# Sampled keys of a paged latent attention: turned by VectorE in 32x32 blocks and scored by 32x32 tiles of TensorE, with work moved between ScalarE, VectorE and GpSimd

## The chip, the core and the metric

The kernel runs on one core of a Trainium2 chip. The metric is the device time of one execution in microseconds (us). A core has TensorE (PE, matmuls and its weight loads, PEld), VectorE (DVE), ScalarE (ACT), GpSimd (POOL) and SyncE (SP), each with its own queue of instructions; they wait for one another through semaphores. PSUM has 8 banks of 512 fp32 values in each of 128 partitions; the kernel calls them K[0] to K[3] and Q[0] to Q[3].

## What is computed

Two layers of a decoder step on 1024 prompt tokens and 8 sequences of 4 sampled tokens. Each layer has latent attention (MLA, 8 heads), an RWKV-7 recurrence (4 heads of 64), a short convolution, an output projection and a mixture of 32 experts. Everything is fp32. The sampled tokens of sequence b attend to 8192 past keys, held in pages of 128 keys with a latent of 128 numbers and a rotary part of 32. Cut to what this change touches:

```python
# sampled attention: ql (8 x 4 x 8 x 128) and qr (.. x 32) against the paged cache
ckv_past = ckv_pages[page_table].reshape(bd, -1, MLA_KV_RANK)   # 8 x 8192 x 128
kr_past = kr_pages[page_table].reshape(bd, -1, MLA_ROPE_DIM)    # 8 x 8192 x 32
s_past = (einsum('bqhc,bkc->bhqk', q_lat, ckv_past)
          + einsum('bqhr,bkr->bhqk', q_rope, kr_past)) * ATTN_SCALE
pr = softmax(concatenate([s_past, s_new], -1), -1)
out = einsum('bhqk,bkc->bqhc', pr[..., :n_past], ckv_past) + ...
# short convolution of the prompt, per channel, width 3
padded = concatenate([buf0, gate_c * u], 1)
y = gate_b * sum(conv_w[j] * padded[:, j:j + t_] for j in range(3))
# recurrence, output side: per-head norm of y, times gain, plus the bonus
bonus = sum(r * k * r_k, -1) * v
out = (yn * lnx_g + lnx_b + bonus) * g
```

## The kernel before

A layer has a projection, a first slot for the sampled rows' recurrence, then eight slots, then the output projection, routing and experts. Slot b does three things at once: the rest of prompt tile b's recurrence, the sampled attention of sequence b, and, from the seam on, prompt tile b+1's preparation together with prompt tile b's causal attention. Its **end** (`end_of_slot`) runs first: TensorE interleaves the last parts of the recurrence (off1, off2, mv, off3, wt, u, st) with the sampled attention. Then comes the **seam** (lora, mlaT, gate and so on of the next tile), then the **body** (`slot`): eight heads of the prompt's scores s0 to s7, with their exponentials, transposes and products, between the steps of the next recurrence. The causal attention grows with the tile, so slot 0 takes about 60 us and slot 6 about 82 us. "Slot 3" below means the stretch from the first sampled key turned for b=3 to the first for b=4. The order on each engine is written out by hand.

The sampled attention of one b is four groups g of 2048 keys, gathered by GpSimd into `ckvr[g]` (128 rows of 16 keys each). In each group:

- TensorE transposes 16 blocks of 128x128 (`keys`, "k0" to "k15" over the four groups), ScalarE copies the results out of Q[1] and Q[2] to kT, 512 columns at a time (`keys` on ScalarE).
- TensorE multiplies the rotary keys (krT, turned by VectorE in 32x32 blocks from krr, step r) by a block diagonal query (qrbd) into Q[0], and adds eight products of the latent query (qcurs, 128x32) with 256 keys each, in four column tiles of 32 (`scores`, step s).
- VectorE adds the window, takes the row maximum (step s), joins it with the earlier maximum across the four column tiles (m), ScalarE takes the exponential (e), VectorE turns the result in 32x32 blocks (T), TensorE multiplies by the values (v), and VectorE accumulates (o).

On VectorE the same stretch holds, of the next tile, kk (the key scaled and squared), of this tile z (two operations that make the bonus and the norm's bias, L2470), u0, u1 and y (copies out of PSUM, L2862 and L2920), off1 (two copies, L2804 and L2805), off3, rows, st, and the prompt tile's convolution (`conv_first`, `conv_rest`: seven operations on 128x256 values). In the body it holds for each head the scores' maximum and a small second instruction, negm (L2974), which multiplies it by minus the scale for ScalarE's exponential; and the grams, masked two heads at a time in 128x128 operations. GpSimd holds roots (rstd and the like), and the gathers of pages and rotary keys: `later_pages` brings the fourth page group and, once VectorE has turned the first two groups' rotary keys, the last two's.

## Time and profile before

| what | us |
| --- | --- |
| runs (three) | 2938.42, 2931.49, 2927.01 |
| median of the runs | 2931.49 |
| span of the profiled execution | 2909.1 |
| TensorE busy | 2670.6 (92%) |
| VectorE busy | 1358.0 (47%) |
| ScalarE busy | 799.2 (27%) |
| GpSimd busy | 648.3 (22%) |

The profiled execution is known by its span only, from its first to its last instruction; the median of the runs is 22.4 us above that. A busy share is a mean over stages: TensorE's 92% says that it is the engine to look at first, not that it sets the time everywhere. The recorded line of a matmul is that of a helper (L964, transposes L961), and that of most two-operand operations of VectorE is L2470, so the names of the operands tell which step is meant. An fp32 matmul leaves two records, a transpose one. "128*32" is the tile of TensorE in rows and columns, "128x256" the moving operand.

### The profile page before, as it was taken

To read this page: it belongs to the slowest core of one execution; us is meant where nothing else is said; L and a number is where in the kernel's file an instruction comes from. 1 tells how busy PE (TensorE), PEld (TensorE's weight loads), DVE (VectorE), ACT (ScalarE), POOL (GpSimd) and SP (SyncE) were. 2 spreads that over 40 slices of the span, in tenths; PEclk is the share of its full clock that TensorE was granted. 3 is DMA by queue.
4 is the path that set the end of the run, shared out by engine and by line. 5 is a ranking of instruction groups with operands and counts; after the bars stand their busy time and mean duration, and the time that the engine had idled before them with its cause. 6 is when DMAs were issued, how large, how long until landed. Compare 5 with 4: busy or idle time off the path is not lost.

```text
span 2909.1 us, 56004 instructions
## 1 busy us (share of the span) xinstructions
PE 2670.6 (92%) x22234; PEld 1459.2 (50%) x22234; DVE 1358.0 (47%) x3828; ACT 799.2 (27%) x1905; POOL 648.3 (22%) x664
## 2 busy tenths in 40 slices
PE   7999899999999959999599998999999997799996
PEld 4445666666655523333244456666666554233332
DVE  4313777666643552222451247677665536322224
ACT  0111455555532101111111014555555210011113
POOL 1000211111100045555320001111111000555543
PEclk9999999999999969999799998999999998899998
DMA  7112433332242549999661133334322326599985
GB/s 299 74 37 53 163 101 109 115 99 83 83 152 81 216 156 360 365 360 329 231 231 58 35 106 116 124 98 121 98 94 80 144 75 265 196 364 357 363 307 209
DMA packets 171814, 502.23 MB, mean 173 GB/s; under 512 B 48388, under 2 KB 89608, under 8 KB 146344
## 3 DMA queue, kind: packets, MB, share of 16 engines
q1 hardware_dynamic: 105624, 321.28, 32.1%
q0 software_dynamic: 50240, 120.23, 12.1%
q10 hardware_dynamic: 15696, 57.15, 4.9%
q8 instruction: 181, 2.97, 0.4%
q14 instruction: 73, 0.60, 0.1%
HBM read 629.15 MB, written 86.89 MB: 246 GB/s over the span
## 4 chain that ended last, share of the span: by engine, by line
PE 78%; DVE 10%; DMA 3%; ACT 3%; DVEq 2%; issue 2%; POOL 0%; POOLq 0%; SPq 0%; ACTq 0%
PE ps L964 70%; PE ps L961 8%; ACT PT L1924 1%; DVE S_all L2972 1%; DVE grams L2470 1%; DMA xd<-o_x 1%; DMA c_x<-xd 1%; ACT S_all L2206 1%; DVEq L2973 1%; DMA l_b<-ybd,dga 1%; DVE negm L2974 0%; DVE uu L2470 0%; DVE krT L2995 0%; DVE r_e L2470 0%; DVE t L2470 0%
## 5 line engine op out<-in xcount | busy, mean ns | idle before, releaser
L964 PE MATMUL ps<-w_slots,xbT 128*64 128x512 f32 (+1 forms) x2048 | 457.4, 599 | 19.0 <-DVE xbT L3429 19.0
L964 PE MATMUL ps<-hT,w_in 128*128 128x512 f32 x896 | 392.0, 595 | 1.2 <-ACT hT L1924 1.2
L867 POOL DMA_INDIRECT xb<-xd,idall x256 | 256.1, 1000 | 144.7 <-issue 80.4
L964 PEld LDWEIGHTS ps<-w_slots,xbT 128*64 128x64 f32 x2048 | 144.0, 138 | 286.7 <-issue 267.4
L964 PEld LDWEIGHTS ps<-hT,w_in 128*128 128x128 f32 x896 | 167.9, 190 | 203.3 <-issue 199.9
L3429 DVE STREAM_TRANSPOSE xbT<-xb 128x1024 f32<-128x1024 f32 x64 | 79.7, 1245 | 357.2 <-DMA xb<-xd,idall 355.0
L964 PE MATMUL ps<-w_out,o_mixT 128*128 128x512 f32 (+1 forms) x640 | 240.0, 555 | 1.4 <-DVE o_h L3235 1.3
L964 PE MATMUL ps<-w_slots,hidT 128*64 128x512 f32 (+1 forms) x1024 | 231.8, 593 | 4.7 <-ACT hidT L1924 2.6
L1924 ACT ACTIVATE kT<-ps 128x512 f32<-128x512 f32 x256 | 138.5, 593 | 128.0 <-PE ps L961 128.0
L964 PE MATMUL ps<-grams 64*64 64x64 f32 (+1 forms) x3536 | 143.1, 228 | 21.9 <-DVE grams L2470 20.0
L964 PE MATMUL ps<-kcat,qcat 96*128 96x512 f32 (+3 forms) x384 | 154.4, 511 | 8.4 <-DVE negm L2974 8.4
L961 PE MATMUL ps<-cst,S_all 128*128 128x128 f32 x832 | 137.7, 285 | 19.8 <-ACT PT L1924 15.7
L964 PEld LDWEIGHTS ps<-w_slots,hidT 128*64 128x64 f32 x1024 | 80.0, 137 | 145.6 <-issue 136.9
L799 POOL TENSOR_TENSOR lnt<-lnt,cst 128x1 f32<-128x1 f32 x36 | 37.3, 1036 | 517.3 <-DVE lnt L2479 517.3
L964 PEld LDWEIGHTS ps<-w_out,o_mixT 128*128 128x128 f32 (+1 forms) x640 | 97.9, 175 | 106.6 <-issue 101.4
L2530 DVE TENSOR_SCALAR stage<-ps,omu 128x512 f32<-128x512 f32 x32 | 24.0, 749 | 270.8 <-PE ps L964 270.8
L1924 ACT ACTIVATE PT<-ps 128x512 f32<-128x512 f32 (+3 forms) x208 | 102.2, 491 | 170.7 <-PE ps L961 132.4
L964 PEld LDWEIGHTS ps<-grams 64*64 64x64 f32 (+1 forms) x3536 | 123.3, 140 | 50.3 <-issue 37.8
L2972 DVE CUSTOM_DVE_ANT_0 S_all<-ps,window 128x256 f32<-128x256 f32 (+7 forms) x128 | 96.5, 754 | 104.9 <-PE ps L964 104.8
L2206 ACT ACTIVATE S_all<-S_all,negm 128x256 f32<-128x256 f32 (+7 forms) x128 | 98.9, 773 | 153.2 <-DVE negm L2974 153.0
L1924 ACT ACTIVATE yb<-ps 128x512 f32<-128x512 f32 x64 | 38.2, 597 | 367.7 <-DMA ybd<-yb 319.6
L961 PEld LDWEIGHTS ps<-cst,S_all 128*128 128x128 f32 x832 | 91.8, 141 | 72.7 <-ACT PT L1924 33.7
(439 smaller groups left out, 4088.4 us busy)
## 6 DMA issues: line engine op xcount, KB each, us to landing
w_slots<-in_w_gu SPq DMA_DIRECT2D x64, 2048.0 KB, 12.6
w_slots<-in_w_dn SPq DMA_DIRECT2D x64, 1024.0 KB, 6.8
ybd<-yb ACTq DMA_DIRECT2D x64, 512.0 KB, 8.3
pd<-stage SPq DMA_DIRECT2D x56, 256.0 KB, 2.5
w_in<-in_w_in SPq DMA_DIRECT2D x6, 2048.0 KB, 24.4
out_y<-c_h ACTq DMA_DIRECT2D x18, 512.0 KB, 2.8
o_mixT<-mixd SPq DMA_DIRECT2D x18, 512.0 KB, 3.7
xd<-o_x ACTq DMA_DIRECT2D x18, 512.0 KB, 2.8
```

The costliest lines, as they stand in the source:

```text
L799: return pool.tensor_tensor(x, x, mh.to_broadcast(shape), ALU.pow)
L867: pool.indirect_dma_start(xb[p % 2][:, 256 * q:256 * q + 256], None, x_quarters, bass.IndirectOffsetOnAxis(ap=idall[:, NE * q + p:NE * q + ...
L961: return pe.transpose(out, in_, ident[s, s])
L964: return pe.matmul(out, lhsT, rhs, start=start, stop=stop, skip_group_check=True)
L1924: return act.activation(out, in_, ACT.Copy)
L2206: self.done(act.activation(S_sb[h % 2][:, :keys], S_sb[h % 2][:, :keys], ACT.Exp, bias=negm[:, h:h + 1], scale=SCALE, accum_out=den[:, h:h ...
L2470: return dve.tensor_tensor(out, x, y, op)
L2530: dve.tensor_scalar(dst[:], src, omu[:, f:f + 1], None, ALU.mult)
L2972: dve.tensor_tensor_reduce(S_sb[h % 2][:, :keys], src, window[:, SEQ - keys:], 1.0, LOW, ALU.add, ALU.max, m8[:, h:h + 1])
L2973: dve.drain()
L3429: dve.transpose(xbT[p % 2][:].rearrange("p (c i t) -> p i c t", c=8, i=4), xb[p % 2][:].rearrange("p (i c t) -> p i c t", c=8, i=4)).then_ ...
```

## The change

The sampled keys are no longer transposed by TensorE. VectorE turns each group's 128x2048 values in 32x32 blocks, in two instructions of 128x1024 (`keys`, steps K0 to K3), into one of two buffers: `kTb0`, or the upper half of `grams`, which the recurrence's matrices leave free because they are laid out anew at 256 columns each. A block turned this way has its 32 latent numbers in one of four row groups of TensorE, so the latent query is held in four shifted copies (`qblk`, made once per layer by sixteen small matmuls and two ScalarE copies, step rep), and a group's scores are 40 matmuls of 32x32 tiles with 256 moving columns: five per output tile (four latent blocks c and the rotary part), over four row tiles j and two halves a. The half a goes to bank Q[a] and to column tile (j + 2a) mod 4. ScalarE's sixteen copies per b are gone. Since the keys' order in half 1 is shifted by two column tiles, VectorE turns the exponentials in three instructions instead of one.

The maxima become minima of the scores times minus the scale, so that negm and its scaling are gone; the masked grams are taken four heads at a time. The prompt tiles' convolution and bonus go to GpSimd (`conv`, `bonus`), kk, u0, u1, y and one copy of off1 to ScalarE. The buffers that the convolution and the grams used change, and with them what SyncE waits for before it loads conv inputs and `w_out` in the last slot (`OUT_GROUPS`). The sampled rows' own convolution stays on VectorE.

The diff, cut:

```diff
-DVE_SATT = "r0 r1 s0 m0 T0 r2 s1 m1 r3 o0 T1 s2 m2 o1 T2 s3 m3 o2 T3 o3".split()
...
+DVE_SATT = "s0 m0 T0 s1 K2 m1 r2 o0 T1 s2 m2 K3 r3 o1 T2 s3 m3 o2 T3 o3".split()
+DVE_ATT = "1s0 1s1 1s2 2K0 1s3 1s4 1s5 1s6 2K1 1s7 1rden 1a 2r0 2r1".split()
+DVE_SATT0 = "r0 K0 r1 K1".split()
...
+        gD, gDT, gN, gM, gX, gXT, gR, gRT, gB, gK = X
+        qrep = grams[:, 4608:4864].rearrange("p (b q) -> p b q", b=NB)
+        kTb = [kTb0[:], grams[:, 2048:4096]]
         wukT = grams[0:64, 0:8 * KR]
...
+            def conv(l, i):
...
+                pool.tensor_tensor(cvp, cvp, cvx[:, 2:4], ALU.mult)
+                pool.drain()
+                pool.tensor_tensor(cvy, cvp[:, :, 0:P], pf(V_CW), ALU.mult)
+                for j in (1, 2):
+                    pool.tensor_tensor(cvt, cvp[:, :, j:j + P], pf(V_CW + 2 * j), ALU.mult)
+                    pool.drain()
+                    pool.tensor_tensor(cvy, cvy, cvt, ALU.add)
+                    pool.drain()
+                pool.wait_ge(mixC_out, 16 * n)
+                pool.tensor_tensor(mixC[:, 2:4], cvy, cvx[:, 0:2, LEAD:], ALU.mult).then_inc(pool_a.sem, pool_a.mark(k, "conv"))
...
+            def bonus(l, i):
...
+                pool.wait_ge(act_a.sem, act_a.at(k, "mv"))
+                pool.tensor_tensor(mix[:].rearrange("p (h v) -> p h v", h=RH), tokm[:, 0:2, :].rearrange("p f (a v) -> p (f a) v", a=2), bc(bon[:], [P, RH, 64]), ALU.mult)
+                pool.drain()
+                pool.tensor_tensor(mix[:], mix[:], rows[:, R_LXB:R_LXB + 256], ALU.add).then_inc(pool_a.sem, pool_a.mark(k, "z"))
...
+                conv(l, b)
                 pool.wait_ge(dve_b.sem, dve_b.at(k, "r0"))
                 ropes(l, b, 2)
                 pool.wait_ge(dve_b.sem, dve_b.at(k, "r1"))
...
+                        pe.wait_ge(dve_b.sem, dve_b.at(("satt", self.l, self.i - 1), "s3"))
                     decay, iclr = (Q[1], Q[2]) if self.seam else (K[1], K[3])
...
+                def scores(self, g, part):
...
+                    if part == 0:
+                        pe.wait_ge(dve_b.sem, dve_b.at(self.k, f"K{g}"))
...
+                        elif self.b:
+                            pe.wait_ge(act_b.sem, act_b.at(("att", self.l, self.b - 1), "R"))
+                        else:
+                            pe.wait_ge(dve_a.sem, dve_a.at(("a", self.l, NPT), "st0"))
+                    else:
+                        pe.wait_ge(dve_b.sem, dve_b.at(self.k, f"r{g}"))
+                    keys = kTb[(g + 1) % 2].rearrange("p (a v c r) -> p a c v r", a=2, v=8, c=4)
+                    for c in ((0, 1), (2, 3, 4))[part]:
+                        for j in range(4):
+                            for a_ in range(2):
+                                i = (j + 2 * a_) % 4
+                                s, out = slice(32 * j, 32 * j + 32), Q[a_][32 * i:32 * i + 32, 0:256]
+                                if c < 4:
+                                    m = mm(out, qblk[s, c, self.b, :], keys[s, a_, c], c == 0, False)
+                                else:
+                                    m = mm(out, qrep[s, self.b, :], krT4[g % 2][s, 256 * a_:256 * a_ + 256], False, True)
+                    if part:
+                        self.done(m, f"s{g}")
...
-                b.both(0)
+                b.scores(0, 0)
                 x.off1()
                 if sample:
                     sample.mixT()
-                b.both(1)
+                b.scores(0, 1)
                 x.off2()
...
+                def kk(self):
+                    for f in range(2):
+                        scale = vec[:, V_KK + f:V_KK + f + 1]
+                        act.activation(kk[:, f, :], xs[:, 2 + f, :], ACT.Copy, scale=scale)
+                        m = act.activation(t1[:, f, :], xs[:, 2 + f, :], ACT.Square, scale=scale)
+                    self.done(m, "kk")
...
+                def u(self, c):
+                    r = slice(CH * c, CH * c + CH)
+                    act.wait_ge(pe_a.sem, pe_a.at(self.k, f"u{c}"))
+                    self.done(cp(pairs(uu)[r], u_ps[r]), f"u{c}")
...
+                def rep(self):
+                    act.wait_ge(pe_a.sem, pe_a.at(self.k, "rep"))
+                    for k in range(2):
+                        m = cp(qblk[:, 2 * k:2 * k + 2].rearrange("p c b q -> p (c b q)"), Q[k])
+                    self.done(m, "rep")
...
+                        mask = cst[:W, self.mbase + k * w:self.mbase + k * w + w].unsqueeze(1).unsqueeze(1).to_broadcast([W, 2, 2, w])
+                        m = tt(dst[:W, :, :w].rearrange("p (f a) t -> p a f t", f=2), gram_ps(q)[:W, :, :, :w], mask, ALU.mult)
...
-                    dve.tensor_tensor_reduce(S_sb[h % 2][:, :keys], src, window[:, SEQ - keys:], 1.0, LOW, ALU.add, ALU.max, m8[:, h:h + 1])
-                    dve.drain()
-                    dve.tensor_scalar(negm[:, h:h + 1], m8[:, h:h + 1], -SCALE, None, ALU.mult).then_inc(dve_b.sem, dve_b.mark(self.k, f"s{h}"))
+                    dve.tensor_tensor_reduce(S_sb[h % 2][:, :keys], src, window[:, SEQ - keys:], -SCALE, HIGH, ALU.add, ALU.min, low[:, h:h + 1])\
+                        .then_inc(dve_b.sem, dve_b.mark(self.k, f"s{h}"))
...
+                def keys(self, g, *halves):
...
+                        dve.wait_ge(ckv_in[g], 16 * (self.l * NB + self.b + 1))
+                        if g >= 2:
+                            dve.wait_ge(pe_b.sem, pe_b.at(self.k, f"s{g - 2}"))
+                        elif self.b:
+                            dve.wait_ge(pe_b.sem, pe_b.at(("satt", self.l, self.b - 1), f"s{g + 2}"))
+                    for a_ in halves:
+                        s = slice(1024 * a_, 1024 * a_ + 1024)
+                        m = dve.transpose(kTb[(g + 1) % 2][:, s], flat(ckvr[g])[:, s])
+                    if 1 in halves:
+                        m.then_inc(dve_b.sem, dve_b.mark(self.k, f"K{g}"))
...
-                    dve.tensor_tensor_reduce(pS[g % 2], Q[0], window[:, 0:512], 1.0, LOW, ALU.add, ALU.max, smg[:, g, 0:1])\
+                    two = [x.rearrange("p (a k) -> p a k", a=2) for x in (pS[g % 2], ps[:, 2048:3072], window[:, 0:512])]
+                    dve.tensor_tensor_reduce(two[0], two[1][:, :, 0:256], two[2], -SCALE, HIGH, ALU.add, ALU.min, smg[:, g, 0:1])\
                         .then_inc(dve_b.sem, dve_b.mark(self.k, f"s{g}"))
...
-                    dve.transpose(pST[g % 2], pS[g % 2]).then_inc(dve_b.sem, dve_b.mark(self.k, f"T{g}"))
+                    p, pT = pS[g % 2], pST[g % 2]
+                    dve.transpose(pT[:, 0:256], p[:, 0:256])
+                    for a_ in range(2):
+                        m = dve.transpose(pT[64 * a_:64 * a_ + 64, 256:512], p[64 - 64 * a_:128 - 64 * a_, 256:512])
+                    m.then_inc(dve_b.sem, dve_b.mark(self.k, f"T{g}"))
...
                 end_of_slot(x, z, b)
             def end_of_slot(x, y, b):
                 x.off1()
+                b.s(0)
                 x.off2()
+                b.max(0)
                 y.sg()
                 y.ssx()
-                y.kk()
-                b.s(0)
-                b.max(0)
                 x.off3()
-                x.z()
+                b.keys(2, 0)
                 b.turned(0)
+                b.s(1)
+                b.keys(2, 1)
+                b.max(1)
                 y.rows()
                 b.ropes(2)
-                x.conv_first()
-                b.s(1)
-                b.max(1)
-                x.u(0)
-                b.ropes(3)
                 b.o(0)
+                x.st(0)
                 b.turned(1)
-                x.st(0)
-                x.conv_rest()
+                b.keys(3, 0)
                 b.s(2)
                 b.max(2)
-                x.u(1)
+                b.keys(3, 1)
+                b.ropes(3)
                 b.o(1)
                 b.turned(2)
                 x.st(1)
                 b.s(3)
-                if x.i + 1 < NPT:
-                    x.y()
                 b.max(3)
-                if x.i + 1 == NPT:
-                    x.y()
                 seam(y, b)
...
+                b.keys(0, 0)
                 x.kk2()
                 x.rkv_begun()
+                b.keys(0, 1)
                 t.s(3)
                 x.rkv_ended()
                 t.s(4)
                 w.hnx()
                 x.gramD()
                 t.s(5)
+                b.keys(1, 0)
                 x.gram23()
                 x.sq(0)
                 t.s(6)
                 x.gram4()
+                b.keys(1, 1)
...
```

TensorE at the start of slot 3's end (any b from 1 on reads the same). Before; `cst,ckvr` are the key transposes, `krT,qrbd` the rotary part and `kT,qcurs` the latent scores, the grams rows are off1 and off2:

```order
L964 MATMUL ps<-grams 64x64 x16
L961 MATMUL ps<-cst,ckvr 128x128 x8
L964 MATMUL ps<-krT,qrbd 128x512
L964 MATMUL ps<-kT,qcurs 32x256 x4
L964 MATMUL ps<-grams 64x64 x16
L961 MATMUL ps<-cst,ckvr 128x128 x8
L964 MATMUL ps<-kT,qcurs 32x256 x4
L964 MATMUL ps<-tokm,grams 64x64 x8
L964 MATMUL ps<-cst,lw 64x2 x4
L964 MATMUL ps<-grams 64x64 x8
```

After; `grams,qblk` or `kTb,qblk` are half of a group's latent scores, `krT,grams` its rotary part:

```order
L1011 MATMUL ps<-grams 64x64 x16
L1011 MATMUL ps<-grams,qblk 32x256 x16
L1011 MATMUL ps<-krT,grams 32x256 x8
L1011 MATMUL ps<-grams 64x64 x16
L1011 MATMUL ps<-kTb,qblk 32x256 x16
L1011 MATMUL ps<-tokm,grams 64x64 x8
L1011 MATMUL ps<-cst,lw 64x2 x4
L1011 MATMUL ps<-grams 64x64 x8
L1011 MATMUL ps<-kTb,qblk 32x256 x16
L1011 MATMUL ps<-krT,grams 32x256 x8
```

The transposes have gone from between the recurrence's steps; the first group's scores stand in two pieces around off1 and are complete ahead of off2.

VectorE in the same end, from the minus-scaled maximum of group 0 (L3017) on. Before:

```order
L3017 TENSOR_SCALAR sneg<-smg 32x1 x4
L2470 TENSOR_TENSOR grams<-grams,ps 128x4x64
L2470 TENSOR_TENSOR mix<-tokm,bon 128x256
L2470 TENSOR_TENSOR mix<-mix,rows 128x256
L3027 STREAM_TRANSPOSE pnT<-pn 32x32
L3028 STREAM_TRANSPOSE PT<-PT 128x512
L2470 TENSOR_TENSOR tmpr<-rowt,cs 128x32
L2470 TENSOR_TENSOR tmpr<-rowt,cs 128x16 x2
L2470 TENSOR_TENSOR rowt<-tmpr 128x32
L2658 SCALAR_TENSOR_TENSOR rowt<-rowt,ss,rows 128x192
L2659 SCALAR_TENSOR_TENSOR rowt<-rowt,ss,rows 128x128
L2995 STREAM_TRANSPOSE krT<-krr 128x512
```

After (helper L2532 is before's L2470; `grams<-ckvr` is half of K2):

```order
L3070 COPY sneg<-smg 32x1 x4
L2698 TENSOR_SCALAR sg<-sg 128x128
L2709 TENSOR_SCALAR ss<-ss 128x2
L2532 TENSOR_TENSOR grams<-grams,ps 128x256
L3045 STREAM_TRANSPOSE grams<-ckvr 128x1024
L3080 STREAM_TRANSPOSE pnT<-pn 32x32
L3082 STREAM_TRANSPOSE PT<-PT 128x256
L3084 STREAM_TRANSPOSE PT<-PT 64x256 x2
L3056 ISA PT,smg<-ps,window 128x512
L3056 ISA smg 128x1
L3045 STREAM_TRANSPOSE grams<-ckvr 128x1024
L3063 COPY smg<-smg 32x1 x3
```

The bonus's two operations have left, two key turns of 128x1024 have come, and T0 stands as two rows of three instructions.

GpSimd, from the gather of the fourth page group (S_all) on. Before:

```order
L826 DMA S_all<-in_cache_ckv,pidx 128x2048
L830 DMA krr<-in_cache_kr,pidx 128x512 x2
L799 TENSOR_TENSOR ss<-ss,cst 128x2
L826 DMA ckvr<-in_cache_ckv,pidx 128x2048
L830 DMA krr<-in_cache_kr,pidx 128x512
```

After (L848 to L857 the convolution, L863 and L865 the bonus):

```order
L870 DMA S_all<-in_cache_ckv,pidx 128x2048
L848 TENSOR_TENSOR cvx<-cvx 128x260
L850 TENSOR_TENSOR cvx<-cvx,vec 128x2x128
L852 TENSOR_TENSOR grams<-cvx,vec 128x256
L854 TENSOR_TENSOR cvx<-cvx,grams 128x2x128
L852 TENSOR_TENSOR grams<-cvx,vec 128x256
L854 TENSOR_TENSOR cvx<-cvx,grams 128x2x128
L857 TENSOR_TENSOR mixC<-cvx 128x256
L874 DMA krr<-in_cache_kr,pidx 128x512 x2
L818 TENSOR_TENSOR ss<-ss,cst 128x2
L863 TENSOR_TENSOR mix<-tokm,bon 128x256
L865 TENSOR_TENSOR mix<-mix,rows 128x256
```

The convolution stands between the fourth page group's gather and those of the last rotary keys, the bonus behind the root of ss.

## Rows read from the trace of the kernel before

**Rows 1.** The profile's page: span, busy time of TensorE, the chain that ended last.

```profile
span 2909.1 us, 56004 instructions
...
PE 2670.6 (92%) x22234; PEld 1459.2 (50%) x22234; DVE 1358.0 (47%) x3828; ACT 799.2 (27%) x1905; POOL 648.3 (22%) x664
...
PE 78%; DVE 10%; DMA 3%; ACT 3%; DVEq 2%; issue 2%; POOL 0%; POOLq 0%; SPq 0%; ACTq 0%
```

**Rows 2.** Windows (us, each engine's busy us): slot 6; slot 3's end and body.

```profile
728.30:810.50 82.20, 75.69 (x1043) 52.93 (x1041) 49.71 (x162) 42.88 (x98) 10.56 (x11) 0.98 0.25 79
517.20:542.60 25.40, 25.40 (x410) 17.30 (x414) 19.53 (x73) 12.93 (x36) 5.14 (x6) 1.00 0.34 86
550.30:572.60 22.30, 21.02 (x276) 13.45 (x274) 19.71 (x65) 13.84 (x31) 1.01 (x1) 1.00 0.15 35
```

**Rows 3.** TensorE's timeline (start us, us), end and body of slot 3, layer 0.

```profile
515.57 0.68 PE L964 MATMUL ps<-cst,grams 64*64 64x64 f32 x16 [0.71 <-DVE grams L2470]
...
517.11 1.09 PE L961 MATMUL ps<-cst,ckvr 128*128 128x128 f32 x8
518.04 1.02 PE L964 MATMUL ps<-krT,qrbd 128*128 128x512 f32 x2
519.00 0.64 PE L964 MATMUL ps<-kT,qcurs 128*32 128x256 f32 x8
519.57 1.15 PE L964 MATMUL ps<-grams 64*64 64x64 f32 x32
...
562.10 0.46 PE L964 MATMUL ps<-l,ta 64*64 64x64 f32 x16
```

**Rows 4.** VectorE's timeline over the same end of slot 3.

```profile
517.23 0.42 DVE L2804 COPY grams<-ps 128x256 f32<-128x256 f32 x1 [1.10 <-issue]
517.57 0.41 DVE L2805 COPY grams<-ps 128x256 f32<-128x256 f32 x1
520.76 0.42 DVE L2470 TENSOR_TENSOR grams<-grams,ps 128x256 f32<-128x256 f32 x1 [2.78 <-PE ps L964]
...
525.23 0.42 DVE L2470 TENSOR_TENSOR mix<-tokm,bon 128x256 f32<-128x256 f32 x1
525.72 0.42 DVE L2470 TENSOR_TENSOR mix<-mix,rows 128x256 f32<-128x256 f32 x1
...
541.90 0.69 DVE L3003 CUSTOM_DVE_ANT_0 PT<-ps,window 128x512 f32<-128x512 f32 x1
```

**Rows 5.** Groups by form (count, busy us, mean ns of one) over the whole run.

```profile
L3429 DVE STREAM_TRANSPOSE xbT<-xb 128x1024 f32<-128x1024 f32 x64 | 79.7, 1245 | 357.2 <-DMA xb<-xd,idall 355.0 <-PE ps L964 2.1
...
L2974 DVE TENSOR_SCALAR negm<-m 128x1 f32<-128x1 f32 x128 | 19.6, 153 | 10.2 <-issue 0.4
```

**Rows 6.** TensorE's waits in 728 to 812 us, slot 6 (us, times, longest).

```profile
PE ps L961 <- ACT PT L1924: 3.2, 5, 1.1
...
PE ps L964 <- DVE negm L2974: 0.9, 1, 0.9
```

**Rows 7.** GpSimd's timeline, end of slot 3.

```profile
511.18 1.01 POOL L826 DMA_INDIRECT S_all<-in_cache_ckv,pidx  x1 [10.22 <-PE ps L961]
...
521.48 0.83 POOL L799 TENSOR_TENSOR ss<-ss,cst 128x2 f32<-128x2 f32 x1 [3.79 <-DVE ss L2648]
```

**Rows 8.** GpSimd's groups by form, over the whole run.

```profile
L899 POOL TENSOR_SCALAR lnl<-lnl 128x1 f32<-128x1 f32 x9 | 2.8, 309 | 17.5 <-ACT l_b L2451 17.3
...
L922 POOL MEMSET xb<- 128x1024 f32 x2 | 1.9, 966 | 0.0
```

**Rows 9.** Windows (behind the engines the granted clock): both slots 0, two stretches.

```profile
327.25:389.47 62.22, 59.04 (x888) 43.23 (x884) 42.73 (x163) 31.45 (x90) 8.69 (x9) 0.89 0.34 104
...
1760.00:1820.00 60.00, 55.13 (x887) 40.13 (x883) 42.49 (x163) 31.30 (x90) 8.67 (x9) 0.97 0.33 103
...
362.00:372.70 10.70, 7.81 (x80) 5.45 (x76) 9.05 (x36) 6.80 (x23) 0.00 (x0) 1.00 0.10 27
372.70:386.40 13.70, 13.40 (x189) 10.30 (x189) 8.45 (x34) 4.41 (x14) 1.01 (x1) 0.50 0.23 59
```

246 lines of the change are left out of this document (110 added, 136 removed).

## The prediction

> **What bounds the kernel now.** First the page: TensorE is busy for 2670.6 of 2909.1 us, VectorE for 1358.0, and the chain that ended last runs 78% on TensorE and 10% on VectorE [rows 1]. That says TensorE, but it is a mean. So next the windows of one slot. In the end of slot 3, where all sampled keys are turned and scored, TensorE is busy for all of 25.40 us, but VectorE has 19.53 us of work in the same stretch [rows 2]. In the early body TensorE has 21.02 and VectorE 19.71 of 22.30 us. A gain on TensorE there is soon stopped by VectorE. In slot 6 VectorE has 49.71 of 82.20 us [rows 2], and TensorE alone sets the time. Last the two timelines of the end of slot 3, for prices and for what waits for what [rows 3, 4].
>
> **TensorE: the keys.** Per group of 2048 keys it now does two times eight transposes (0.93 us to the next start each), the rotary product (0.96) and eight products of 256 columns (two times 0.57) [rows 3]: 4.0 us, 16 us per b. After: 40 matmuls, 80 records of 256 columns. One record of 256 columns is 0.24 us (the rotary product is two of 512 in 0.96) to 0.285 (0.57 for two rounds of four column tiles) [rows 3]. If the eight matmuls of one c run together, a group is five rounds of two records, 2.4 to 2.85 us; I take 2.6, 10.4 per b, so 5.6 us are saved per slot, some 90 us in 16 slots. For eight at once speaks the row of l,ta: 16 records of 64*64 tiles, on two row groups and two column groups, end 0.46 us after their start, while one after another they would need 16 times a quarter of 0.24, 0.96 us. Two row groups that write one bank are the diagonal tiles of the row `cst,grams`: its 16 records take 0.68 us to the last end, again under 0.96 [rows 3]. The Trainium skill, TensorEngine Tiling (Array Packing), "Gotcha 1: PSUM Pressure", says that different row tiles cannot access the same PSUM bank at once; here four row tiles write Q[0] and four Q[1]. By that rule the sum would be the last rival's below; by the grams row it stays 2.6.
>
> **VectorE: the end of a slot.** It takes 25.36 us from off1 (517.23) to the end of s3 (541.90 + 0.69) [rows 4]. Removed: kk 2, the bonus 2, the convolution 7, u0, u1 and one off1 copy, 14 operations of 128x256, each 0.34 us to the next start (517.23 to 517.57) or 0.49 where a drain stands between (525.23 to 525.72) [rows 4]; at 0.44, 6.2 us. Added: four turns of 128x1024 (K2, K3). That form takes 1.245 us [rows 5], less the 0.08 by which 0.42 overlaps the next start, 1.17: 4.7 us. T0 to T2 become three instructions each: three times 0.34 for one of 128x512 (0.69 as s3 has it [rows 4], less 0.08), +0.4 each, 1.2 us. Work is then 0.3 us less. Waits: the largest, 2.78 us for off2 [rows 4], shrinks, since TensorE has 1.6 us of scores (three fifths of 2.6) between off1 and off2 where it had 2.46 (517.11 to 519.57) [rows 3], and s0 with its 0.7 moves into it: -1.4. The end is about 23.7 us for both engines: TensorE's 25.4 less 5.6 is 19.8, so VectorE sets it, and of TensorE's 5.6 us only 1.7 arrive. Then y's copy goes (0.34), the last T costs 0.4 more, and TensorE's lora waits for s3, with ScalarE's new copies ahead of its own: I give back 0.7 and let the body start 0.9 us earlier (bounds 0 and 2.1).
>
> **VectorE: the body.** K0 and K1 of the next b add 4.7 us. Eight negm go, 0.153 us each [rows 5] and a drain, 1.2 to 2.4, taken at 1.8. The masks are six instructions fewer for as many elements: 0 to six times 0.153, taken at 0.5. Net +2.4; idle is 22.30 less 19.71, 2.6 us [rows 2], most of it in drains, and I let it cover 0.6 (bounds 0 and 2.4). Early bodies (slots 0 to 3) grow by 1.8 us, since TensorE waits there for VectorE's scores and grams. In slots 4 to 6 VectorE has room, and TensorE's waits for negm (0.9) and for PT behind the exponentials (3.2 over five) [rows 6] become shorter: slot 4 -0.7 with its end, slots 5 and 6 -2.0 each.
>
> **The rest.** Before slot 0 nothing earlier can hold K0 and K1 of b = 0 (2.3 of 4.7 uncovered) and rep is sixteen matmuls, 1.9 us at four together, 1.5 uncovered: +3.8 per layer. The last slot starts its outputs 1.4 earlier. ScalarE loses its copies of keys and gains eight small ones per slot: nothing. GpSimd's convolution starts at 512.2, after the gather at 511.18 (1.01) [rows 7]. A 128x256 operation is not in the trace: below stands 0.31 us (128x1), above 0.97 (128x1024) [rows 8]; I take 0.7, seven in 5 us, to 517.2. The root of ss came at 521.48 after 3.79 us idle, with two gathers between [rows 7]; it is due when VectorE reaches rows, near 527, so this is hidden. The changed w_out loads wait for earlier things than their use; nothing.
>
> **Sum.** Per layer 3.8, four times (1.8 - 0.9) = 3.6, -0.7, -4.0, -1.4: +1.3; two layers +2.6. On the span of 2909.1 that is 2911.7; the median of the runs stands 22.4 above the span and I keep that distance: 2934 us. My own range for this case is 2918 to 2948: bodies from +1 to +2.4, ends from -0.3 to -1.7.
>
> **Rivals.**
> 1. *Faster: VectorE's new work fits into its waits.* If the body's idle covers 2 us instead of 0.6, early slots come out at -0.5 to -1.5, and if the end gives its 1.7 whole, per layer: 2 - 4 times 1.3 - 3 times 3 - 1.4 = -14, two layers -28: 2906; at most -40. For it: five or six waits in the end are for TensorE itself, which is now early, and 90 us come off the busiest engine. Against it: VectorE has 42.73 and 42.49 us of work in the slots 0 of about 61 [rows 9], and the change takes none of it away.
> 2. *Slower: TensorE's clock falls.* From 362.0 TensorE was busy for 7.81 of 10.70 us at full clock, and the next 13.70 us were granted 0.50, the 1.2 GHz level [rows 9]. Slot 0 of layer 0 with a mean of 0.89 took 62.22 us, that of layer 1 with 0.97 took 60.00: 2.2 us [rows 9]. Slot ends that were 100% busy become 19.8 of 23.7, 84%, with small tiles in place of 128*128 transposes. If each of 15 ends draws such a fall, +33: 2967. Against it: 84% is above the 73% ahead of that fall, and the body behind it is full.
> 3. *Slower: only four tiles at a time* (one row group after another, as kT,qcurs does now with its four column tiles [rows 3]). Then 4.8 us a group, 19.2 per b against 16: TensorE's end is 28.6 us, and from 4.0 us a group on TensorE decides. Sixteen ends +2.9, early bodies +1.8, late ones less: +57, 2988.
> 4. *Slower: GpSimd is late.* At 2 us an operation the convolution ends at 526.2, the two gathers and the root near 529.5; rows and r2 wait 3.5 us, in 16 slots 56: 2990. It decides from 1.4 us an operation on, far over the 0.97 of four times the size. The Trainium skill, SBUF — State Buffer, "SBUF: two separate sides", says that VectorE with two SBUF operands and GpSimd share a pair of ports, held for a whole instruction, the other blocked. By that rule each of nine operations could stand still for one of VectorE's 0.42 us, or hold it up; that is less than what the mechanism needs.
> 5. *One row tile per bank.* Two matmuls at a time: 9.6 us a group, 38.4 per b, +22.4 in 16 slots: 3290. The grams rows stand against it.
>
> **Chances.** Forecast 0.35, rival 1 0.34, rival 2 0.15, rival 3 0.08, rival 4 0.07, rival 5 0.01. 0.5% is 15 us, about what a measurement of this kernel can tell from no change. Faster (under 2917): 0.35, rival 1 and the forecast's tail; within: 0.35; slower: 0.30. The range takes in rival 1 with its bounds and rival 2: 2892 to 2972, leaving out rivals 3 to 5 and some tails.
>
> **What would show it.** Right: in the changed profile TensorE's busy time is down by 70 to 100 us while the span stays; 32 records of `kTb,qblk` (half a group's latent part) take about 1 us to the next start; the end of slot 3 from off1 to s3 lasts 23 to 24.5 us, with VectorE at 20 of them; TensorE gains waits for s, K or grams; the early body's 22.3 us are up to about 24; slots 5 and 6 are shorter by 2. Wrong: a slot end near 22 us and bodies as before (rival 1), a granted clock of 0.5 at slot ends (rival 2), those 32 records in 1.9 us or more (rivals 3, 5), the last rotary gathers later than 526 or GpSimd operations over 1.4 us (rival 4).

## The result, and the profile after

The changed kernel takes 3007.38 us (median of four runs, 2997.47 to 3019.72) against 2930.73 of the kernel before in the same session (2927.01 to 2938.42). The ratio is 1.0268, interval 1.0234 to 1.0302: slower by 2.7%, 77 us, above the upper end of the range, 2972 us. The prediction was wrong. Times and ratios are those of executions in the fast state; one execution of the kernel with fill matmuls took 3937.62 us at a granted clock of 0.643 and is left out.

The page after, with the lines that answer to [rows 1]: span and instructions, the engines, TensorE's granted clock in 40 slices in tenths, the chain that ended last.

```profile
span 3003.5 us, 61674 instructions
...
PE 2671.2 (89%) x25242; PEld 1440.0 (48%) x25242; DVE 1433.0 (48%) x3610; ACT 706.6 (24%) x1773; POOL 744.7 (25%) x808
...
PEclk9999889999999969999799998999999998799998
...
PE 67%; DVE 16%; issue 5%; ACT 4%; DVEq 4%; DMA 3%; POOL 1%; another core or an unknown queue 0%; POOLq 0%; ACTq 0%; SPq 0%
```

VectorE's share of the chain is up from 10% to 16% and TensorE's down from 78%, yet TensorE's busy time is the same, 2671.2 against 2670.6, although it has less to do. Most of what it saved came back as slower matmuls: the mean granted clock is 0.943 against 0.965, and 340.7 us of the span are granted 0.50 against 205.1. The stretches of [rows 2] after (slot 3's end and body; then slot 4's end whole and in two parts; the columns are TensorE, its loads, VectorE, ScalarE, GpSimd, granted clock, DMA share, GB/s):

```profile
537.68:563.95 26.27, 22.73 (x578) 15.45 (x579) 20.80 (x68) 8.09 (x29) 11.67 (x15) 0.94 0.50 142
572.47:596.92 24.45, 21.09 (x274) 13.31 (x272) 22.70 (x56) 13.90 (x31) 1.01 (x1) 1.00 0.13 32
606.90:635.10 28.20, 24.83 (x582) 15.64 (x582) 20.65 (x68) 8.19 (x29) 11.67 (x15) 0.88 0.43 132
621.60:628.40 6.80, 3.75 (x104) 2.28 (x97) 6.33 (x19) 1.38 (x4) 1.87 (x2) 1.00 0.70 241
628.40:635.20 6.80, 6.80 (x116) 3.90 (x105) 3.35 (x10) 0.38 (x1) 0.95 (x1) 0.50 0.36 128
```

Slot 3's end was 25.4 us with TensorE busy throughout and is 26.27 with 3.5 us idle. Its body went from 22.3 to 24.45, VectorE at work for 22.70 of it. In slot 4 TensorE is busy for 3.75 of 6.80 us at full clock, and the next 6.80 us are granted 0.50, the 1.2 GHz level.

All 16 slots, by the starts of VectorE's operations in each profiled execution (us; end, seam, body and tail run from off1 to s3's end, to the prompt's s0, to the end of its s7, and to the next off1; "half" is time at 0.50):

| part | before | after | difference | forecast |
|---|---|---|---|---|
| ends (16) | 406.3 | 443.0 | +36.7 | -27 |
| seams (16) | 121.2 | 134.6 | +13.4 | +13 |
| early bodies (8) | 163.1 | 186.0 | +22.9 | +14 |
| late bodies (6) | 183.0 | 183.5 | +0.5 | -4 |
| last bodies (2) | 166.8 | 164.2 | -2.6 | -1 |
| tails (14) | 153.8 | 157.5 | +3.7 | 0 |
| half clock, in ends | 0.0 | 81.4 | | |

The forecast's column splits its slots: 1.7 off each end, of which 0.8 goes back in the seam; 1.8 onto each early body; the late and last slots with their 0.9 taken out. The differences add up to +74.4 (rounding aside), and what lies before the first off1 adds 2.8: +77, the measured difference. The two spans differ by 94.4. The other 17.2 lie in what follows the last bodies (output, routing, experts): 1384.8 us before and 1402.0 after. The eleven kernels below have 1395 to 1415 there, the folds alone 1403.3, so before's profiled execution was short there by chance, as the medians say too.

### The profile page after: what moved, and what is told of

Its sections match the earlier page's. It is cut to its first block, busy times and chain, and to the rows that moved or that the text cites. A ratio compares the mean times of both kernels' runs of the same rounds, so it can differ in the third digit from the quotient of the medians.

```text
span 3003.5 us, 61674 instructions
## 1 busy us (share of the span) xinstructions
PE 2671.2 (89%) x25242; PEld 1440.0 (48%) x25242; DVE 1433.0 (48%) x3610; ACT 706.6 (24%) x1773; POOL 744.7 (25%) x808
## 4 chain that ended last, share of the span: by engine, by line
PE 67%; DVE 16%; issue 5%; ACT 4%; DVEq 4%; DMA 3%; POOL 1%; another core or an unknown queue 0%; POOLq 0%; ACTq 0%; SPq 0%
PE ps L1011 62%; PE ps L1008 4%; DVE grams L3045 2%; DVE kTb L3045 1%; DVE S_all L3011 1%; DVE PT L3084 1%; ACT PT L1973 1%; DVEq L3061 1%; DMA xd<-o_x 1%; ACT S_all L2281 1%; DMA c_x<-xd 1%; DVE krT L3033 1%; DVE PT L3056 1%; DVE grams L2532 1%; DVE sneg L3070 0%
## 5 line engine op out<-in xcount | busy, mean ns | idle before, releaser
L818 POOL TENSOR_TENSOR gn<-gn,cst 128x4 f32<-128x4 f32 (+1 forms) x36 | 36.9, 1024 | 424.4 <-DVE gn L2974 366.3
L1011 PE MATMUL ps<-kTb,qblk 32*32 32x256 f32 x2048 | 99.6, 463 | 44.2 <-DVE kTb L3045 42.7
L2281 ACT ACTIVATE S_all<-S_all,low 128x256 f32<-128x256 f32 (+7 forms) x128 | 98.9, 773 | 162.6 <-DVE low L3011 162.3
L1008 PE MATMUL ps<-cst,S_all 128*128 128x128 f32 x576 | 103.0, 288 | 34.0 <-ACT PT L1973 31.8
L3469 DVE SCALAR_TENSOR_TENSOR gt<-gt,ps 128x256 f32<-128x256 f32 x64 | 27.0, 421 | 200.4 <-ACT gt L2474 179.5
## 6 DMA issues: line engine op xcount, KB each, us to landing
w_in<-in_w_in SPq DMA_DIRECT2D x6, 2048.0 KB, 25.4
```

The source lines that it names most:

```text
L818: return pool.tensor_tensor(x, x, mh.to_broadcast(shape), ALU.pow)
L1008: return pe.transpose(out, in_, ident[s, s])
L1011: return pe.matmul(out, lhsT, rhs, start=start, stop=stop, skip_group_check=True)
L2281: self.done(act.activation(S_sb[h % 2][:, :keys], S_sb[h % 2][:, :keys], ACT.Exp, bias=low[:, h:h + 1], scale=-1.0, accum_out=den[:, h:h + ...
```

## The experiments

Eleven kernels were run. Each is the changed kernel with one edit (the last with two), but for the folds alone, which is the kernel before with one part of the change. This table gives the ratio to the kernel before with its 95% interval and the same sums as above. The sums are those of one profiled execution each, which lies up to 12 us from its kernel's median.

| run | median us | ratio | ends | early | late | tails | half, in ends |
|---|---|---|---|---|---|---|---|
| after | 3007.38 | 1.0268 (1.0234-1.0302) | 443.0 | 186.0 | 183.5 | 157.5 | 81.4 |
| no turns | 2878.61 | 0.9821 (0.9796-0.9846) | 378.8 | 150.9 | 175.7 | 150.5 | 12.5 |
| one turn of T | 2974.33 | 1.0149 (1.0127-1.0171) | 416.0 | 187.4 | 183.9 | 158.1 | 61.5 |
| fill matmuls | 2970.63 | 1.0141 (1.0116-1.0166) | 415.7 | 186.7 | 183.6 | 159.2 | 3.4 |
| keys back | 2910.12 | 0.9922 (0.9896-0.9948) | 408.3 | 150.5 | 175.7 | 154.4 | 0.0 |
| folds alone | 2912.30 | 0.9921 (0.9907-0.9935) | 393.9 | 150.9 | 175.7 | 170.8 | 0.0 |
| conv and bonus on VectorE | 3077.45 | 1.0482 (1.0462-1.0502) | 488.0 | 184.2 | 183.4 | 178.4 | 158.7 |
| K3 earlier | 2963.45 | 1.0093 (1.0074-1.0112) | 398.8 | 187.4 | 183.5 | 160.2 | 0.0 |
| four tiles at once | 3054.69 | 1.0402 (1.0376-1.0428) | 493.8 | 192.1 | 183.8 | 163.7 | 27.3 |
| no K0, K1 | 2958.05 | 1.0061 (1.0036-1.0086) | 437.4 | 150.5 | 175.9 | 152.0 | 66.1 |
| no K2, K3 | 2937.92 | 1.0002 (0.9984-1.0019) | 374.2 | 186.0 | 183.7 | 156.4 | 0.0 |
| K3 earlier and fill | 2963.63 | 1.0085 (1.0055-1.0114) | 404.0 | 188.1 | 183.6 | 158.8 | 3.4 |

### Without the turns of the keys

```diff
-    pe.wait_ge(dve_b.sem, dve_b.at(self.k, f"K{g}"))
-    keys = kTb[(g + 1) % 2].rearrange(...)
+    pe.wait_ge(ckv_in[g], 16 * (self.n + 1))
+    keys = flat(ckvr[g]).rearrange(...)
```

with the steps K0 to K3 taken out of VectorE's program.

> The changed kernel with the eight key turns per b left out (TensorE reads the gathered keys as they lie, so that the sampled scores are those of other keys; everything else is as changed). Theory A, VectorE's chain: it loses 9.4 us of VectorE work in each of 16 slots; TensorE no longer waits for K3 (2.7 us a slot in the changed trace) and the early bodies shrink by 2 to 3 us: the end from off1 to s3 falls from 26.3 to about 22.5, and the ratio to before is 0.965 to 0.985. Theory B, the clock: TensorE's work in the ends is the same small tiles, packed into less time; the half-clock stretches in the slots (about 136 us in the changed trace, about 20 before) stay, the ends stay above 24, and the ratio stays above 1.0.

Measured: 2878.61 us, 0.9821. The 128 turns, 150 us of VectorE's time by their mean of 1.17 us, cost 1.0268 less 0.9821 of 2931 us, 131 us: seven eighths of their length. Both disputed places shrink, the ends by 64 us and the early bodies by 35. An end is then 23.7 us (378.8 over 16), not the 22.5 that was expected.

### One turn instead of three for the exponentials

```diff
-    dve.transpose(pT[:, 0:256], p[:, 0:256])
-    for a_ in range(2):
-        m = dve.transpose(pT[64 * a_:64 * a_ + 64, 256:512], p[64 - 64 * a_:128 - 64 * a_, 256:512])
+    m = dve.transpose(pT, p)
```

> The changed kernel with each turn of the exponentials (T0 to T3) as one instruction of 128x512 again instead of three (half 1 of the values then meets other keys; nothing else differs). In the changed trace the three take 1.33 us to the next start, the one takes 0.61 to 0.66. Theory A: four times 0.7 in 16 slots is 45 us of VectorE's chain, of which two thirds show: ratio to before about 1.015 instead of 1.027. Theory B: VectorE's time is not what was lost; ratio 1.025 or more.

Measured: 2974.33 us, 1.0149: 35 us for 64 splits, 0.54 each. VectorE's timeline after, with the three instructions of one split (start, length), and the two forms over the whole run (count, busy us, mean ns):

```profile
543.46 1.24 DVE L3045 STREAM_TRANSPOSE grams<-ckvr 128x1024 f32<-128x1024 f32 x1
544.62 0.16 DVE L3080 STREAM_TRANSPOSE pnT<-pn 32x32 f32<-32x32 f32 x1
544.71 0.39 DVE L3082 STREAM_TRANSPOSE PT<-PT 128x256 f32<-128x256 f32 x1
545.12 0.89 DVE L3084 STREAM_TRANSPOSE PT<-PT 64x256 f32<-64x256 f32 x2
546.04 0.69 DVE L3056 CUSTOM_DVE_ANT_0 PT<-ps,window 128x512 f32<-128x512 f32 x1
```

```profile
L3084 DVE STREAM_TRANSPOSE PT<-PT 64x256 f32<-64x256 f32 x128 | 56.3, 440 | 1.7
...
L3082 DVE STREAM_TRANSPOSE PT<-PT 128x256 f32<-128x256 f32 x64 | 27.4, 428 | 25.6 <-ACT fade L2307 25.5
```

The split takes 544.71 to 546.04, 1.33 us, against 0.61 for one instruction: +0.7, where +0.4 was priced. A turn on half the partitions (these two also move the blocks to the other half) takes as long as one on all of them, 440 and 428 ns.

### Matmuls that only keep TensorE busy

```diff
+    def fill(n):
+        for _ in range(n):
+            mm(Q[2], ident[:], window[:, 0:512], True, True)
...
+                fill(1)
                 b.v(1)
...
+                fill(2)
                 b.scores(3, 0)
```

> The changed kernel with three matmuls of 128x128 by 512 columns added in each end of a slot, one ahead of v1 and two ahead of the scores of group 3, where TensorE waits for T1 and K3; their result goes to an unused bank and is never read. About 0.96 us each at full clock. Theory A: they lie in waits (0.7 and 2.3 us in slot 3) and change nothing: ratio 1.025 to 1.035. Theory B: TensorE's clock stays up in more of the ends; half-clock time in the slots falls from about 136 us to under 70, the ends with a fall lose their extra 1.6 us: ratio 1.010 to 1.020.

Measured: 2970.63 us, 1.0141. More work for TensorE made the kernel 37 us faster. The clock's mean is 0.959 and the ends have 3.4 us at half clock instead of 81.4. The end of slot 4 with it:

```profile
601.20:627.70 26.50, 24.95 (x588) 15.82 (x592) 20.78 (x68) 8.19 (x29) 11.40 (x15) 1.00 0.45 140
```

At full clock this end is still 26.50 us where before had 25.4, though the three fills are in it. So the clock is part of the loss; that it is not the root is shown by "K3 earlier" below.

### The sampled keys as before, the rest of the change kept

In outline:

```diff
-def scores(self, g, part): ...   # 32x32 tiles over kTb
+def keys(self, g): ...           # eight 128x128 transposes per pair
+def scores(self, h): ...         # and the products over kT, with qrbd
-    b.keys(0, 0) ... b.keys(3, 1)   # VectorE's turns
```

> The changed kernel with the keys as before (TensorE transposes, ScalarE copies, scores in one bank, T in one instruction), and all the rest of the change kept: folded minus scale, masks four at a time, convolution and bonus on GpSimd, kk, u0, u1, y on ScalarE. Theory A and B both say that the loss sits in the keys: ratio 0.985 to 1.0, early bodies 2 us shorter than before's, ends at TensorE's 25.4 less nothing, clock as before. A rival C, that the moves to GpSimd and ScalarE cost (shared ports, ScalarE's queue ahead of the key copies): ratio over 1.01.

Measured: 2910.12 us, 0.9922. The keys' part of the change is worth +101 us (1.0268 less 0.9922), all of the loss and more. Without the turns it is 0.9821 less 0.9922, -30 us, with the splits of T in it: that is what arrives of TensorE's 90 us, against 131 us for the turns. TensorE's busy time differs by 52 us between these two kernels (2670.9 and 2619.3), with nearly the same time at half clock (206.7 and 208.5 us), so part of the 90 was never saved; see below. Windows of this kernel, the end and the body of slot 3:

```profile
512.10:537.55 25.45, 25.45 (x410) 17.24 (x414) 14.61 (x58) 15.18 (x44) 11.69 (x15) 1.00 0.45 127
545.28:566.58 21.30, 20.77 (x274) 13.39 (x272) 18.36 (x52) 13.84 (x31) 1.01 (x1) 1.00 0.16 37
```

TensorE fills the end again, and VectorE stands for 10.8 of 25.45 us: the convolution and the bonus rows that left it bought nothing there.

### The folded maxima and masks alone, on the kernel before

```diff
-    dve.tensor_tensor_reduce(..., src, window[:, SEQ - keys:], 1.0, LOW, ALU.add, ALU.max, m8[:, h:h + 1])
-    dve.drain()
-    dve.tensor_scalar(negm[:, h:h + 1], m8[:, h:h + 1], -SCALE, None, ALU.mult)
+    dve.tensor_tensor_reduce(..., src, window[:, SEQ - keys:], -SCALE, HIGH, ALU.add, ALU.min, negm[:, h:h + 1])
```

and the masks over four heads in one instruction, as in the change.

> The kernel before with two small parts of the change alone: minus the scale folded into the prompt's maxima (negm gone) and the grams masked four heads at a time. Keys, convolution, bonus and all copies as before. The run with the keys back gained 0.8%, all of it in the bodies (17.9 us against 19.4 from s0 to s7 in slot 1), where only these two parts act. Theory: they alone bring the whole of it, ratio 0.990 to 0.995. Rival: the moves to GpSimd and ScalarE helped as well by clearing VectorE in the ends (10 us of its idle there); then these two bring less, ratio 0.996 to 1.0.

Measured: 2912.30 us, 0.9921. The early bodies are 12.2 us shorter (1.5 apiece) and the late ones 7.3 (1.2 apiece). Two of before's bodies, slot 0 and slot 6 of layer 0, were partly at half clock; pairs without any give 0.9 to 1.6 for an early body and 0.9 to 1.1 for a late one. The ends are 12.4 us shorter, but the tails take 17.0 back; why was not looked into. The whole is as much as the kernel with the old keys gains. It and that kernel beat both the kernel before and the changed one.

### Convolution and bonus back on VectorE

```diff
-POOL_SEAM = "1conv 2rstd 1z 2kkn 1hn"
+POOL_SEAM = "2rstd 2kkn 1hn"
...
+                x.z()
                 y.rows()
...
+                x.conv_first()
+                x.conv_rest()
```

> The changed kernel with the prompt tiles' convolution (seven operations) and bonus (two) back on VectorE. Theory A (VectorE sets the slot's end): nine operations at 0.34 to 0.49 us, 3.9 us in each of 15 to 16 ends, most of it in the chain: +35 to +60 us on the changed kernel, ratio 1.04 to 1.047. Rival (GpSimd's operations take VectorE's ports, so that the move saved little): ratio 1.025 to 1.032.

Measured: 3077.45 us, 1.0482: 63 us more than the changed kernel, 3.9 per slot for nine operations of 0.42 us. Half clock in the ends rises from 81.4 to 158.7 us, so part of the 63 us is the clock's. Work that cost nothing to have on VectorE where TensorE filled the end (406.3 us before, 408.3 with the keys back) costs as much as its length here.

### The last keys turned before s2

```diff
-DVE_SATT = "... o0 T1 s2 m2 K3 r3 o1 T2 s3 m3 o2 T3 o3".split()
+DVE_SATT = "... o0 T1 K3 s2 m2 r3 o1 T2 s3 m3 o2 T3 o3".split()
...
-                b.keys(3, 0)
+                b.keys(3, 0, 1)
                 b.s(2)
                 b.max(2)
-                b.keys(3, 1)
```

> The changed kernel with both halves of K3 turned ahead of s2 and m2 on VectorE, instead of one half ahead and one behind. Theory A1 (the loss is VectorE's total work): TensorE waits less for K3 and more for what s2 and m2 release: ratio 1.024 to 1.030. Rival A2 (the loss is this order): TensorE's 2.7 us of waiting for K3 per slot shrinks to about 1 and with it some of the falls of the clock: ratio 1.010 to 1.020.

Measured: 2963.45 us, 1.0093. No work is added or removed, and 51 us go. TensorE's waits after had this row (us in total, times, longest):

```profile
PE ps L1011 <- DVE kTb L3045: 42.7, 16, 2.9
```

In this run no such row is among its largest; in its place TensorE waits 17.5 us in 16 slots for s2, and half clock in the ends goes from 81.4 to 0. TensorE's wait ahead of the last group's scores and the end of slot 4 in this run (start, length; then the window):

```profile
549.90 1.10 PE L1011 MATMUL ps<-kTb,qblk 32*32 32x256 f32 x32 [0.83 <-DVE smg L3056]
```

```profile
599.66:624.38 24.72, 22.40 (x586) 14.63 (x583) 20.57 (x68) 8.19 (x29) 11.67 (x15) 1.00 0.48 150
```

### Four tiles at once instead of eight

```diff
-    i = (j + 2 * a_) % 4
+    i = j
```

with the single turn of T that goes with it. Both halves of a row tile then use the same column tile.

> The changed kernel with both halves of the keys on the diagonal tiles (row group j to column group j, halves still in two banks), so that only four different tiles of the array are in use instead of eight; T is one instruction again, since the order is natural. If eight at once are what made the scores fast, 32 records of kTb,qblk take about 2.05 us to the next start instead of 1.03, a group 5.1 instead of 2.6, 10 us more on TensorE per slot: the end becomes TensorE's, near 29 us, and the ratio is 1.03 to 1.05 in spite of the shorter T, with the clock back up at 0.96. If two movings into one row group do not run together anyway, the records keep 1.03 us and the ratio is that of the single T, about 1.015.

Measured: 3054.69 us, 1.0402. TensorE's timeline after and in this run, over the same 32 matmuls (the next row's start ends them):

```profile
540.15 1.10 PE L1011 MATMUL ps<-kTb,qblk 32*32 32x256 f32 x32
541.18 0.68 PE L1011 MATMUL ps<-tokm,grams 64*64 64x64 f32 x16
```

```profile
549.78 1.97 PE L1011 MATMUL ps<-kTb,qblk 32*32 32x256 f32 x32
551.68 0.27 PE L1011 MATMUL ps<-tokm,grams 64*64 64x64 f32 x2
```

1.03 us against 1.90: the changed kernel does run eight tiles together, with four row tiles writing each bank. Against the run with one turn of T, which differs from it in the placing alone, the ends are 77.8 us longer, 4.9 each: 30.9 us, where rival 3 had 28.6.

### Half of the turns left out, either half

```diff
+UNTURNED = (0, 1)        # or (2, 3)
...
+    if g in UNTURNED:
+        pe.wait_ge(ckv_in[g], 16 * (self.n + 1))
+    else:
         pe.wait_ge(dve_b.sem, dve_b.at(self.k, f"K{g}"))
```

> The changed kernel with the turns of groups 0 and 1 left out (K0 and K1, which lie in the slots' bodies; the scores of these groups are then those of other keys). By the slot tables the early bodies take 186 us in all in the changed kernel and 151 without any turns, the late ones 183.5 and 176. If bodies and ends add up, this run's early bodies are back at about 151 and its ends stay near 440: 43 us off the changed kernel, ratio about 1.012. If the bodies' delay was only passed on (what waits in the body then waits in the end), the ratio stays over 1.02.

> The changed kernel with the turns of groups 2 and 3 left out (K2 and K3, in the slots' ends; scores of other keys in these groups). All turns together were worth 128 us; if the bodies' share is 43, this one is 75 to 85: the ends go from 443 us in all to about 385, no clock falls in them (81 us at half clock in the changed kernel), early bodies stay at 186, ratio about 1.0. If the clock falls hang on small tiles and not on the waiting, half-clock time in the ends stays at 50 us or more and the ratio over 1.01.

Measured: 2958.05 us, 1.0061, without K0 and K1, and 2937.92, 1.0002, without K2 and K3. The first are worth 61 us: 35.5 in the early bodies, 7.6 in the late ones, the others in ends and tails. The second are worth 78 us, 69 of them in the ends, where they also take the wait for K3 and all half clock with them. Together 139, close to the 131 of both at once. K0 and K1 also carry the half clock of the early bodies: 32.5 us after, 32.6 without K2 and K3, 0.1 without K0 and K1.

### The last keys earlier, and fill matmuls

The edit of "K3 earlier" with `fill(1)` ahead of v1 and of the last group's scores.

> The changed kernel with K3 turned ahead of s2 and one filling matmul of 512 columns ahead of v1 and one ahead of the scores of group 3, unread. With K3 earlier alone the ends had no half-clock time left (81 before it) and 55 us of it stood in the bodies. Theory: what K3's order gave back (50 us) and what the filling matmuls gave back (36 us) are largely the same clock falls and waits, so together they are little better than K3's order alone: ratio 1.004 to 1.012. Rival: they add up, ratio under 1.0.

Measured: 2963.63 us, 1.0085 (1.0055 to 1.0114), the same as K3 earlier alone. The two cures, 51 and 37 us, don't add: the fills repaired a clock that falls only because TensorE waits.

## Why the prediction was wrong, point by point

**TensorE's price of the keys was right for the first group only.** There it is 1.03 us for 32 records, as above, and 1.45 us for the other 48, the rotary part with them (537.57 to 539.02):

```profile
537.57 1.09 PE L1011 MATMUL ps<-grams,qblk 32*32 32x256 f32 x32
538.45 0.64 PE L1011 MATMUL ps<-krT,grams 32*32 32x256 f32 x16
539.02 1.15 PE L1011 MATMUL ps<-grams 64*64 64x64 f32 x32
```

2.5 us, where 2.6 was taken and [rows 3] had 4.0. The rotary part takes 0.57 us here and in the first group of every slot. In the later groups it is mostly longer, as in the last one of slot 3 with K3 earlier, 1.16 us (552.90 to 554.06) at full clock:

```profile
552.01 1.10 PE L1011 MATMUL ps<-kTb,qblk 32*32 32x256 f32 x32 [0.16 <-DVE krT L3033]
552.90 1.23 PE L1011 MATMUL ps<-krT,grams 32*32 32x256 f32 x16
554.06 1.08 PE L1011 MATMUL ps<-ckvr,PT 128*32 128x128 f32 x32
```

So the term "TensorE's 25.4 less 5.6 is 19.8" failed as well. In that kernel, with no half clock in its ends, TensorE is busy for 354.1 us in 16 ends, 22.1 each: 3.3 us came off, and 2.3 of the 5.6 did not. What the rotary parts take beyond 0.57 us is 26.1 us in its 16 slots, 1.6 of those 2.3. Why they do, and what the rest is, stays open. The run with four tiles at once measures what rivals 3 and 5 supposed, and it is another kernel. The Trainium skill's rule on row tiles in one bank (TensorEngine Tiling (Array Packing), "Gotcha 1: PSUM Pressure") does not show as a slowdown for tiles that write different partitions of the bank; the measurement decides.

**The turns' length was right,** 1.24 us or 1.17 to the next start, as [rows 5] said of the same form. The split of T was mis-sized, +0.7 and not +0.4: the sum took 0.34 to the next start, a copy's, for each of the three, and they take 0.41, 0.46 and 0.46 (544.71, 545.12, 546.04). Over three T in an end that is 0.9 us.

**The step that failed: "The end is about 23.7 us for both engines", with "Waits: ... -1.4".** Measured: 27.7 on the mean of 16, 4.0 more than forecast and 2.3 more than before, 64 us of the error. The sum added VectorE's operations and let its waits for TensorE shrink. The one that it named did: the 2.78 us ahead of off2 are 1.20 ahead of s0 (539.31) and 0.21 ahead of off2 (540.22). It did not follow the new edge the other way, TensorE waiting for K3, whose second half stands in VectorE's queue behind s2 and m2. TensorE's row and VectorE's rows over the same stretch after:

```profile
558.28 1.10 PE L1011 MATMUL ps<-kTb,qblk 32*32 32x256 f32 x32 [2.27 <-DVE kTb L3045]
```

```profile
553.66 1.25 DVE L3045 STREAM_TRANSPOSE kTb<-S_all 128x1024 f32<-128x1024 f32 x1
554.83 0.65 DVE L3056 CUSTOM_DVE_ANT_0 PT<-ps,window 128x512 f32<-128x512 f32 x1
...
556.34 0.62 DVE L3070 COPY sneg<-smg 32x1 f32<-32x1 f32 x4
556.98 1.25 DVE L3045 STREAM_TRANSPOSE kTb<-S_all 128x1024 f32<-128x1024 f32 x1
...
563.26 0.69 DVE L3056 CUSTOM_DVE_ANT_0 PT<-ps,window 128x512 f32<-128x512 f32 x1 [1.92 <-PE ps L1011]
```

Between K3's halves lie 2.15 us of s2 and m2; TensorE waits 2.27 us for the second half; then it scores, and VectorE waits 1.92 us for those scores at s3. Each engine waits for the other in turn, so neither sets the time alone, and a sum over one of them comes out short. TensorE's waits of this kind are 42.7 us in 16 slots. Moving one step in the order took 44 us from the ends: that shows it. Nor would 23.7 have held with the turns: without K2 and K3, 4.7 us of VectorE's work in an end, the end still takes 23.4 us (374.2 over 16), TensorE being busy for 21.9 of it. The order was in the listing of the change, and the forecast named "TensorE gains waits for s, K or grams" as something to look for without pricing it.

**Rival 2, TensorE's clock, came on top, mostly as a consequence.** It had a chance of 0.15 and +33 us. The fill matmuls took away 78 us of half clock in the ends and 37 us of time. The forecast tied the fall to the busy share of the whole end and to small tiles. The runs tie it to TensorE's waiting: K3 earlier and no K2, K3 have the same small tiles and none of it in the ends, and no turns has 12.5 us. The end of slot 4 falls behind a stretch that was 3.75 of 6.80 us busy; the forecast's argument, 84% over the end, was a mean over such stretches. With the fills and the old order the ratio is 1.0141; with the order mended and no fills, 1.0093. The clock explains most of why TensorE's busy time, forecast 70 to 100 us lower, did not move: no turns, with the same scoring, has 2619.3. The rest was never saved: the rotary parts above are much of it.

**Even with K3 earlier the end is 24.9 us, not 23.7.** By its price the split of T is 0.9 of the 1.2 us; no run had both K3 earlier and one turn of T. TensorE's 22.1 us of work, not 19.8, leave it less room than the sum had.

**The body: "I let it cover 0.6".** Measured +2.9 per early body against +1.8. Most of the excess is the clock again, which the sum left out of the body. The early bodies have 32.5 us at half clock after, 10.7 before, and none with the folds alone. Slot 2's body, after and with the fills (whose edit lies in the ends), shows what such a fall costs:

```profile
504.21:528.14 23.93, 19.98 (x258) 13.18 (x256) 21.73 (x56) 12.70 (x31) 1.01 (x1) 0.93 0.22 33
496.40:519.20 22.80, 18.57 (x256) 12.11 (x254) 21.48 (x56) 12.32 (x31) 1.01 (x1) 1.00 0.22 34
```

At full clock the whole change adds 2.2 us there (20.56 before) and 2.2 in slot 3 (22.24 to 24.45), near the 1.8. Luck has a part in that: the folds give 1.4 and 0.9 in these two bodies where 2.3 was taken (1.8 for negm and 0.5 for masks), and against them the turns cost 3.6 and 3.2 of their 4.7 us, so that 1.1 and 1.5 was covered and not 0.6. The two errors cancel in part. Without K0 and K1 the half clock of these bodies is 0.1 us; that it comes from TensorE's waiting for VectorE, as in the ends, is argued.

**The late bodies: "In slots 4 to 6 VectorE has room".** It has 7.05 us idle in slot 6's body after, and still the turns cost 1.3 us per late body (183.5 less 175.7, over 6), more than the folds gain at full clock, 0.9 to 1.1. (Slot 6 of layer 0 was 35.01 us before, with 3.4 at half clock, and 33.38 in layer 1; with 33.38 in both, the table's +0.5 would be +2.1.) VectorE's timeline around the prompt's scores in slot 6, after and with the old keys:

```profile
808.85 1.24 DVE L3045 STREAM_TRANSPOSE grams<-ckvr 128x1024 f32<-128x1024 f32 x1
...
813.32 1.05 DVE L3011 CUSTOM_DVE_ANT_0 S_all<-ps,window 128x896 f32<-128x896 f32 x1
```

```profile
768.21 1.09 DVE L3023 CUSTOM_DVE_ANT_0 S_all<-ps,window 128x896 f32<-128x896 f32 x1 [0.96 <-PE ps L1009]
```

With the old keys VectorE waits 0.96 us for TensorE there; with a turn of 1.24 in its queue it comes without a wait, that is late. Room on the mean of a body does not cover an instruction that is longer than the gap it falls into. From the head before it to this one are 5.48 us after and 4.24 with the old keys. That this is the whole of the 1.3 in each late body is argued from this place, not shown.

**The seams** were priced at +0.8 per slot and came out at +0.84, which is partly luck: 7.4 us of them are at half clock, and with K3 earlier, with none, they are 130.0 us, +0.55 per slot. **GpSimd** was late nowhere (rival 4): its rows after, the convolution's second and last operations, the next rotary gather, and the second of the two bonus rows:

```profile
537.96 0.62 POOL L850 TENSOR_TENSOR cvx<-cvx,vec 128x256 f32<-128x256 f32 x1 [4.53 <-issue]
...
541.72 0.64 POOL L857 TENSOR_TENSOR mixC<-cvx 128x256 f32<-128x256 f32 x1
542.50 1.00 POOL L874 DMA_INDIRECT krr<-in_cache_kr,pidx  x1
...
550.87 0.72 POOL L865 TENSOR_TENSOR mix<-mix,rows 128x256 f32<-128x256 f32 x1 [4.77 <-issue]
```

Operations of 128x256 take 0.61 to 0.75 us, as the 0.7 taken. With the wait of 4.53 us the convolution ends at 542.36, and the rotary gathers behind it (542.50 and 543.80) are still 6 us ahead of r2 at 550.52. The Trainium skill's shared ports (SBUF — State Buffer, "SBUF: two separate sides") were not put to the test: in this end VectorE has no operation of 128x256 with two SBUF operands beside them.

**Rival 1** (faster) fell with the same two steps: it needed 2 us of cover in the body, and 1.1 to 1.5 was there at full clock.

In sum: of an error of 74 us (77 measured, 2.6 forecast) the ends are 64, the early bodies 8.5, the late bodies 4.5, the tails 3.7 and the seams 0.6; the last bodies take off 1.6, and the time before the first slots, +2.8 where +7.6 was forecast, 4.8. By cause, K3's place with the clock that it draws is 51. The folds, the split of T and TensorE's saving were sizes that were off, and the clock of the early bodies was left out. Of the 90 us to be taken from the busiest engine 52 came off its busy time and 30 arrive; of 150 added to the second busiest 131 arrive.
